# A two-block transformer layer on one core: another order of work at four norms, and the second attention's last product in three fp32r products

## The chip, the cores and the metric

The kernel runs on one core of one Trainium2 chip, as one launch. The metric is the device time of that launch in microseconds (us); the median of three runs of the kernel before is 2761.93 us (2761.17 to 2762.11). Everything is computed on 256 tokens with a model width of 2048.

## The reference, cut to what matters

Two blocks follow each other. Each mixes tokens, adds a normed result to the residual x, and runs a gated feed-forward (FFN). The norms and the second block's linear attention are what the change touches:

```
def rms_norm(x, g):                    # mean of squares over the 2048 features
    y = xf * lax.rsqrt(mean(xf * xf) + 1e-6);  return y * g
# first block
h = rms_norm(x, mix_pre_g); ... mixed = concat(o_da, o_hg) @ w_out
x = x + rms_norm(mixed, mix_post_g)
h = rms_norm(x, cross_pre_g); qx = h @ w_cq ...          # norm 1 (cq)
x = x + rms_norm(o @ w_co, cross_post_g)
h = rms_norm(x, ffn_pre_g); gate, up = h @ w_ffn_in      # norm 2 (Fg0)
x = x + rms_norm((silu(gate) * up) @ w_ffn_out, ffn_post_g)
# second block
h = rms_norm_2(x, norm_mix_pre); z = h @ w_in            # norm 3 (R0)
A = masked, decayed scores of q and k (gla);  o = A @ v  # the "second attention"
o = rms_norm_2(o, gla_norm) * silu(r); y_b = o @ w_branch_b
mixed = (gates0 * y_a + gates1 * y_b) @ w_out
x = x + rms_norm_2(mixed, norm_mix_post)
h = rms_norm_2(x, norm_ffn_pre); f = (silu(h @ wg) * (h @ wu)) @ w_ffn_down   # norm 4 (Hg0)
x = x + rms_norm_2(f, norm_ffn_post)
```

So four times a post norm is added to x and the new x is normed for the next projection: these four places are "the later norms" 1 to 4.

## The kernel before, in words

**The stream of weights.** All weights are cut into slots of 128 x 1024 numbers, in the order in which they are used. SyncE loads slot i into one of four RAW buffers; ScalarE copies it to RH as fp32r (the high part, `s_hi`); VectorE subtracts and writes the rest to RL (the low part, `s_lo_v`). For six slots (the second one, index 1, of cq, co0, co1, Fg0, R0 and Hg0) GpSimd makes the low part instead (`on_pool`). TensorE multiplies each slot in three fp32r products (low of tokens by high of weights, high by low, high by high): 12 matmuls of 512 columns for most slots. RH and RL have four buffers, so the high part of slot i can be made only when slot i-4 is multiplied. `upto(n)` on an engine means "do the slots up to n"; the engines run three slots ahead (LA).

**Order.** Each engine's instruction list is written out by hand in the functions `tensor`, `scalar`, `vector`, `gpsimd`; each engine works through its own list strictly in order and waits at semaphores. Work beside the stream is a "side task" with ticks in slots (`yield at`): `sides.behind(t)` emits all side work due up to tick t, after the engine's own work of that slot.

**A later norm n.** The last four slots of the projection before it (`tail_of`) are multiplied for token block b = 0 (tokens 0 to 127) and then for b = 1 (`by_token_halves`). When b = 0 is done, ScalarE squares its last quarter, VectorE makes the mean (`post_mean`), GpSimd the power -0.5, and VectorE adds four quarters of 512 features to x (`post_add`, `s_xv`). TensorE turns x over by transposes into eight steps (`half_turns`, steps 0 and 1 for b = 0, 2 and 3 for b = 1, both with features 0 to 1023; 4 to 7 with features 1024 to 2047 of both blocks). For each step ScalarE writes the high part of the turned x (`half_highs`, `s_nhi`) and VectorE the low part (`half_lows`, `s_nlo`). `by_token_head` multiplies the first four slots of the next projection, called f to f+3 below, in an order that follows these steps, and `rest_by_token` the slots f+4 to f+7, one after the other. On ScalarE, `row_task(n)` then squares x in four halves of 1024 (ticks f, f+1, f+2, f+2.5) for the norm's scale; by the lists, three of them stand ahead of the high part of slot f+6.

**The second attention's last product** (`gla_out_task`). Scores ATT2, AX2 and values V2 are plain fp32; eight outputs (4 heads, 2 token blocks) come from 12 fp32 matmuls of 512 columns, in two lumps in slots of R1. ScalarE and VectorE copy them out.

**Level tasks.** The causal decays of both attentions are made in levels L = 0, 1, 2, ... (`level_plan`): spans and factors on VectorE, exp on ScalarE, small products on TensorE (`e.mul`), a masked copy on VectorE (`e.take`).

Of the kernel before, what the change touches and what calls it, by code (L numbers as in the profile page):

```python
# [7 lines left out]
F32 = mybir.dt.float32  # L8
# [5 lines left out]
P = 128  # L14
D = 2048
T = 256
# [151 lines left out]
def build(nc, A, out, scratch):  # L168
    ctx = ExitStack()
    with ctx:  # L170
# [106 lines left out]
        on_pool = {i for n in ("cq", "co0", "co1", "Fg0", "R0", "Hg0") for i in groups[n][1:2]}  # L277
# [47 lines left out]
        s_sg = sem("branch_gate_ready")  # L325
        s_go, s_gov, s_goa = sem("gla_out_multiplied"), sem("gla_out_copied_by_vector"), sem("gla_out_copied_by_scalar")
# [33 lines left out]

        low_sum = {}
# [24 lines left out]
        NORM_BANKS = []  # L386
        for n, name in enumerate(NORMED):
            head = unit[name, 0]
            tail = unit[NORM_AFTER[n][-1], 0] if n else [6, 7]
            NORM_BANKS.append(head + [b for b in range(8) if b not in head + tail] + tail)  # L390
# [41 lines left out]
        GLA_END = last("V0")  # L432

# [9 lines left out]
        def level_plan(todo, at, period, fac, banks, base, squeeze):  # L443
# [3 lines left out]
            for L in todo:  # L447
# [9 lines left out]
                else:  # L457
                    e.mul, e.take = squeeze(at), squeeze(at + 2)
# [46 lines left out]
        V2 = U(0, 2).rearrange("p (b n) -> p b n", b=2)  # L505
# [59 lines left out]
        def tensor(g):  # L565
# [103 lines left out]
            def by_token_halves(name, H, L, n=None):  # L669
# [42 lines left out]
            def half_turns(n, s0, s1):  # L712


                for s in range(s0, s1):
# [6 lines left out]
                    for blk in range(cols.start // P, cols.stop // P):  # L722
                        g.wait_ge(s_xv, 8 * (n - 1) + 4 * blk + chunks[0] // 4 + 1)
# [5 lines left out]
            def by_token_head(name, H, L, n):  # L729
# [41 lines left out]
                rest_by_token(name, H, L, 8, lambda k: (s_nlo, 8 * n + k // 2 + 1))  # L771

            def rest_by_token(name, H, L, k, ready):
                banks = unit[name, 0]
                for i in groups[name][k // 2:]:
                    wait_low(i)
# [14 lines left out]

            def norm(n):
                banks = NORM_BANKS[n]

                def turn_over(i, blk):
                    if blk == 0:
                        for name in NORM_AFTER[n]:
                            if banks[i] in unit[name, 0]:
                                g.wait_ge(*free_of[name, 0][unit[name, 0].index(banks[i])])
                    g.wait_ge(s_xv, 8 * (n - 1) + 4 * blk + i // 2 + 1)  # L800
                    for c in range(2):
                        cc = 2 * i + c
                        t = turn(PS[:, banks[i], c * T + blk * P:c * T + blk * P + P], X[:, blk, cc * P:cc * P + P])
                    if blk:
                        t.then_inc(s_tr, 1)

                assert n not in HALVED
                for blk in range(2):
                    for i in range(8):
                        turn_over(i, blk)  # L810
# [224 lines left out]
            def gla_out_task():  # L1035
                at = lambda h, s: ATT2[:, (2 * h + s) * P:(2 * h + s) * P + P]
                yield GLA_OUT
                g.wait_ge(s_free_a, read_a["V3"])
                for j in range(2):
                    g.wait_ge(s_lv_v[j], gla_done[j][0])  # L1040
                for blk in range(2):
                    for h in range(4):
                        vs, o = slice(512 * h, 512 * h + 512), PS[:, 4 + h, :]
                        if blk == 0:
                            mm(o, at(h, 0), V2[:, 0, vs], True, True).then_inc(s_go, 1)
                        else:
                            if h % 2:
                                g.wait_ge(s_goa, h // 2 + 1)
                            else:
                                g.wait_ge(s_gov, h // 2 + 1)  # L1050
                            mm(o, at(h, 1), V2[:, 1, vs], True, False)
                            mm(o, AX2[:, h * P:h * P + P], V2[:, 0, vs], False, True).then_inc(s_go, 1)
                    yield GLA_OUT + 1
# [86 lines left out]
        def scalar(g):  # L1140
# [62 lines left out]
            def half_norm(n, half):  # L1203


                H, f = NORM_HOME[n][0], first(NORMED[n])
                upto(f + 1)
                if n == 2:
                    half(1, [2])
                g.wait_ge(s_slot, last(HOME_READ[n]) + 1)  # L1210
# [7 lines left out]
            def norm(n, H, next_slot):  # L1218
                gain = PRE_GAIN[n]
                g.wait_ge(s_slot, last(HOME_READ[n]) + 1)  # L1220
                for i in range(8):
                    if i == 2:
                        upto(next_slot + 1)
                    g.wait_ge(s_tr, 8 * (n - 1) + i + 1)
                    for c in range(2):
                        t = act(H[:, 2 * i + c, :], PS[:, NORM_BANKS[n][i], c * T:c * T + T], scale=gcol(gain, 2 * i + c))
                    t.then_inc(s_nhi, 1)
# [32 lines left out]
            def row_task(n):  # L1260
                at = first(NORMED[n]) + (0, 4)[n == 0]
                ss = stat(f"row_ssq{n}", 4).rearrange("p (b h) -> p b h", b=2)
                for q, (half, b) in enumerate(X_HALF):
# [5 lines left out]
                    else:  # L1269
                        g.wait_ge(s_xv, 8 * (n - 1) + 4 * b + 2 * half + 2)  # L1270
# [154 lines left out]

            def gla_out_task():
                ss = stat("gla_ssq", 8)
                for blk in range(2):
                    yield GLA_OUT + blk
                    for h in (1, 3):  # L1430
                        g.wait_ge(s_go, 4 * blk + h + 1)
                        act(O2[:, blk, h, :], PS[:, 4 + h, :]).then_inc(s_goa, 1)
# [24 lines left out]
            def mixed_task():  # L1457
                for j in range(4):
# [10 lines left out]
                          pool_task(), gla_out_task(), branch_gate_task(0), branch_gate_task(1), mixed_task(), row_task(4), hidden_task(0), hidden_task(1))  # L1469
# [156 lines left out]
            for j in range(4):  # L1626

                def second_values(banks):
                    for x in range(2):
                        g.wait_ge(s_lv_v[x], gla_done[x][0])  # L1630
# [1014 lines left out]
```

## Time and profile before

| | |
|---|---|
| median of 3 runs | 2761.93 us |
| the profiled execution | 2762.22 us |
| its span | 2760.4 us |
| TensorE matmul busy | 2739.2 us, 99% |
| VectorE busy | 1813.2 us, 66% |
| ScalarE busy | 1338.3 us, 48% |
| GpSimd busy | 76.0 us, 3% |
| granted TensorE clock, mean | 0.998 of 2.4 GHz |

The span is what lies between the first and the last instruction of the execution; the execution's own time is 1.8 us longer. TensorE is the engine to look at: the other engines matter only where TensorE waits for them. A timeline row gives start, length, instruction and count, and in square brackets the idle time of the engine ahead of it with what ended it.

### The profile page before, as it was taken

How to read it: one execution, taken by the hardware profiler on the slowest of the kernel's cores; microseconds unless marked ns; L12 is line 12 of the kernel's file. 1: busy time of each engine (PE TensorE's matmuls, PEld its weight loads, DVE VectorE, ACT ScalarE, POOL GpSimd, SP SyncE). 2: the span in 40 equal slices, each digit the busy share in tenths (PEclk: the TensorE clock that was granted, in tenths of full speed). 3: DMA queues.
4: the chain of work that ended last, by engine and by line, in shares of the span. 5: the costliest groups of instructions: out<-in, count | busy, mean ns of one | idle time of the engine just before them, and what ended most of it. 6: DMA issues, size and time to landing. Idle time of an engine off the chain costs nothing.

```text
span 2760.4 us, 35257 instructions
## 1 busy us (share of the span) xinstructions
PE 2739.2 (99%) x14278; PEld 2272.6 (82%) x14278; DVE 1813.2 (66%) x2294; ACT 1338.3 (48%) x1604; POOL 76.0 (3%) x61
## 2 busy tenths in 40 slices
PE   9999999999999999999999999999999999999998
PEld 7888887888888888887888887888888888888887
DVE  6778865575556655766679754868667546656575
ACT  5666544664444434445545545544454444443443
POOL 0000000110000000000002000000010000000000
PEclk9999999999999999999999999999999999999999
DMA  8555455556655665554655555565655555565655
GB/s 324 195 165 175 155 186 181 174 186 203 193 190 190 199 195 192 194 188 161 223 177 179 182 190 195 189 212 182 206 192 189 198 193 194 186 202 189 197 190 160
DMA packets 145540, 529.21 MB, mean 192 GB/s; under 512 B 16305, under 2 KB 16737, under 8 KB 144737
## 3 DMA queue, kind: packets, MB, share of 16 engines
q1 hardware_dynamic: 142528, 514.71, 57.0%
q0 software_dynamic: 2560, 12.07, 1.2%
q8 instruction: 113, 1.85, 0.3%
q14 instruction: 51, 0.41, 0.0%
q10 hardware_dynamic: 288, 0.16, 0.0%
HBM read 524.78 MB, written 2.11 MB: 191 GB/s over the span
## 4 chain that ended last, share of the span: by engine, by line
PE 95%; DVE 2%; ACT 2%; issue 1%; DMA 0%; POOL 0%; DVEq 0%; SPq 0%; POOLq 0%; ACTq 0%
PE PS L568 95%; PE PS L571 1%; ACT RH L1145 1%; DVE RL L1652 1%; ACT A_HL L1145 1%; DVE AR L1652 0%; ACT SP L1145 0%; DVE AR L2136 0%; DMA RAW<-in_stream 0%; DVE X L1658 0%; DVE A_HL L1658 0%; ACT B_HL L1145 0%; DVE AR L1891 0%; POOL ST L2406 0%; DVE AR L1655 0%
## 5 line engine op out<-in xcount | busy, mean ns | idle before, releaser
L1652 DVE TENSOR_TENSOR RL<-RAW,RH 128x1024 fp32r<-128x1024 f32 x954 | 1159.3, 1225 | 837.3 <-ACT RH L1145 835.2
L1145 ACT ACTIVATE RH<-RAW 128x1024 fp32r<-128x1024 f32 (+1 forms) x962 | 1013.9, 1057 | 1129.5 <-PE PS L568 1101.6
L568 PE MATMUL PS<-RH,A_HL 128*128 128x512 f32 x4096 | 1271.9, 391 | 4.3 <-ACT A_HL L1145 1.4
L568 PEld LDWEIGHTS PS<-RH,A_HL 128*128 128x128 f32 x4096 | 768.5, 188 | 168.4 <-issue 6.5
L568 PE MATMUL PS<-RH,B_HL 128*128 128x512 f32 x2624 | 810.6, 390 | 0.4 <-DVE RL L1652 0.3
L568 PE MATMUL PS<-RL,A_HL 128*128 128x512 f32 x2048 | 793.4, 390 | 0.0
L568 PEld LDWEIGHTS PS<-RH,B_HL 128*128 128x128 f32 x2624 | 492.5, 188 | 103.9 <-DVE RL L1652 1.3
L568 PE MATMUL PS<-RL,B_HL 128*128 128x512 f32 x1312 | 509.0, 389 | 0.0
L568 PEld LDWEIGHTS PS<-RL,A_HL 128*128 128x128 f32 x2048 | 384.9, 188 | 78.8 <-issue 0.5
L568 PEld LDWEIGHTS PS<-RL,B_HL 128*128 128x128 f32 x1312 | 246.2, 188 | 50.6
L568 PE MATMUL PS<-A_HL,RH 128*128 128x512 f32 (+1 forms) x912 | 221.5, 394 | 2.0 <-DVE A_HL L1658 2.0
L568 PEld LDWEIGHTS PS<-A_HL,RH 128*128 128x128 f32 (+1 forms) x912 | 165.6, 189 | 36.0 <-issue 3.2
L2112 DVE STREAM_TRANSPOSE AR<-AR 32x256 f32<-32x256 f32 x352 | 153.3, 436 | 4.9
L568 PEld LDWEIGHTS PS<-A_HL,RL 128*128 128x128 f32 (+1 forms) x912 | 118.0, 192 | 6.4 <-DVE RL L1652 0.8
L568 PE MATMUL PS<-A_HL,RL 128*128 128x256 f32 (+1 forms) x912 | 122.7, 287 | 0.0
L1652 DVE TENSOR_TENSOR AR<-PS,AR 128x512 f32<-128x512 f32 (+2 forms) x106 | 77.2, 740 | 44.2 <-ACT AR L1145 26.3
L1652 DVE TENSOR_TENSOR AR<-AR 128x512 f32<-128x512 f32 (+3 forms) x145 | 100.9, 733 | 0.4
L2406 POOL TENSOR_TENSOR ST<-ST,NEG 128x1 f32<-128x1 f32 (+2 forms) x21 | 26.1, 1241 | 2020.9 <-DVE ST L1658 1725.7
L1145 ACT ACTIVATE AR<-PS,ST 128x512 f32<-128x512 f32 (+1 forms) x82 | 50.6, 666 | 57.9 <-PE PS L568 55.9
L1145 ACT ACTIVATE AR<-AR 128x1024 f32<-128x1024 f32 (+2 forms) x64 | 65.0, 1029 | 13.4 <-DVE AR L1652 9.0
L1145 ACT ACTIVATE AR<-PS 128x512 f32<-128x512 f32 (+2 forms) x48 | 31.6, 665 | 73.3 <-PE PS L568 69.2
L568 PEld LDWEIGHTS PS<-AR 128*32 128x32 f32 (+5 forms) x1938 | 48.7, 119 | 14.6 <-issue 10.5
(117 smaller groups left out, 832.5 us busy)
## 6 DMA issues: line engine op xcount, KB each, us to landing
RAW<-in_stream SPq DMA_DIRECT2D x959, 512.0 KB, 4.2
X<-in_x SPq DMA_DIRECT2D x4, 512.0 KB, 7.0
AR<-in_mem SPq DMA_DIRECT2D x4, 512.0 KB, 6.8
AR<-in_mem_turned SPq DMA_DIRECT2D x4, 512.0 KB, 5.1
AR<-in_b_branch_gates POOLq DMA_DIRECT2D x4, 512.0 KB, 6.3
AR<-in_b_branch_gates POOLq DMA_DIRECT2D x2, 1024.0 KB, 8.6
out_x<-X SPq DMA_DIRECT2D x8, 256.0 KB, 2.7
AR<-in_x_turned SPq DMA_DIRECT2D x3, 512.0 KB, 8.3
```

The source lines that it names most:

```text
L568: return g.matmul(o, l, r, start=start, stop=stop, skip_group_check=True)
L571: return g.transpose(o, i, ident)
L1145: return g.activation(o, i, f, bias=bias, scale=scale, accum_out=accum)
L1652: return g.tensor_tensor(o, a, b, f)
L2112: t = g.transpose(dst[32 * fq:32 * fq + 32, :, :, tq, :], src[32 * tq:32 * tq + 32, :, :, fq, :])
L2406: return g.tensor_tensor(o, i, NEG[:, 0:k], ALU.pow)
```

## The change

- **Norms, TensorE.** The transposes of steps 4 to 7 no longer stand together in the head: steps 4 and 5 come late in the head, steps 6 and 7 between slots f+4 and f+5. The order of the head's products changes; at norm 3 steps 0 and 1 come one slot later.
- **Norms, ScalarE.** The first high parts no longer wait for the end of wo3 (norm 1) but for its head. The square of the last quarter of b = 1 comes between the high parts of slots f+2 and f+3 (norm 3: behind both). The high parts of steps 4 to 7 were one run behind slot f+5; now step 4 stands behind slot f+4, steps 5 to 7 behind slot f+5.
- **Norms, VectorE.** The additions to x are cut into first two quarters, third and last, with weights' low parts between; at norm 3 quarters of both blocks alternate.
- **GpSimd** makes low parts in co0 and co1 only; the four others go to VectorE.
- **Second attention.** Scores and values are split into high and low (in B_HL), and each fp32 matmul becomes three fp32r matmuls: 36 in all, head by head, in slots of V1, V2, V3 and R1.
- **Level L = 0**: `e.mul` one tick later, `e.take` half a tick later.
- **mixed_task**: the last two groups of VectorE's 32 x 32 transposes at ticks 2 and 3 instead of 1.5 and 2.

```diff
-        on_pool = {i for n in ("cq", "co0", "co1", "Fg0", "R0", "Hg0") for i in groups[n][1:2]}
+        on_pool = {i for n in ("co0", "co1") for i in groups[n][1:2]}
...
+        def quarter_added(n, b, c):
+            order = [(k, q) for k in range(2) for q in range(4)]
+            if n == 3:
+                order = [(0, 0), (0, 1), (1, 0), (1, 1), (0, 2), (1, 2), (0, 3), (1, 3)]
+            return 8 * (n - 1) + order.index((b, c)) + 1
...
-        HOME_READ = [None, "wo3", "cq", "Fu10", "yb3"]
+        HOME_READ = [None, head_of("wo3")[-1], last("cq"), last("Fu10"), last("yb3")]
...
-                    e.mul, e.take = squeeze(at), squeeze(at + 2)
+                    e.mul, e.take = squeeze(at + 1), squeeze(at + 2.5)
...                                          # tensor, by_token_halves and by_token_head
-                        if n in HALVED and b and i == tail_of(name)[2]:
+                        if n in HALVED and b and i == tail_of(name)[2 + (n == 3)]:
                             half_turns(n, 0, 2)
...
                 highs(0, range(4))
-                low_tokens(0, range(4))
-                half_turns(n, 2, 3)
-                low_weights(0, range(2))
+                low_tokens(0, range(2))
+                if n != 3:
+                    half_turns(n, 2, 3)
+                low_tokens(0, range(2, 4))
+                low_weights(0, range(1))
+                if n == 3:
+                    half_turns(n, 2, 3)
                 half_turns(n, 3, 4)
+                low_weights(0, range(1, 2))
+                highs(1, range(4))
+                low_tokens(1, range(4))
+                low_weights(1, range(2))
                 low_weights(0, range(2, 4))
-                for ms in (range(2), range(2, 4)):
-                    if ms[0]:
-                        half_turns(n, 4, 8)
-                    highs(1, ms)
-                    low_tokens(1, ms)
-                    low_weights(1, ms)
+                half_turns(n, 4, 6)
+                low_weights(1, range(2, 4))
...                                          # rest_by_token
                 for i in groups[name][k // 2:]:
+                    if k == 10:
+                        half_turns(n, 6, 8)
                     wait_low(i)
...                                          # scalar, half_norm
                 half_highs(n, H, 0, 2)
+                upto(f + 2)
+                if n == 3:
+                    upto(f + 3)
+                half(1, [3])
                 upto(f + 3)
-                half(1, [3])
                 half_highs(n, H, 2, 4)
+                upto(f + 4)
+                half_highs(n, H, 4, 5)
                 upto(f + 5)
-                half_highs(n, H, 4, 8)
+                half_highs(n, H, 5, 8)
...                                          # vector, half_norm (after)
+                for step in ("early", "sum", "mean", "first_quarters"):
+                    half(0, step)
+                upto(f)
+                if n != 3:
+                    half(0, "last_gain")
+                    half(0, "third_quarter")
+                    half(0, "last_quarter")
+                    half(1, "early")
+                half_lows(n, 0, 1)
                 half(1, "sum")
+                half_lows(n, 1, 2)
+                if n == 3:
+                    half(0, "last_gain")
                 half(1, "mean")
                 half(1, "first_quarters")
+                upto(f + 2)
+                half_lows(n, 2, 4)
                 upto(f + 3)
+                if n == 3:
+                    half(0, "third_quarter")
+                half(1, "third_quarter")
                 upto(f + 4)
+                half_lows(n, 4, 5)
+                half(1, "last_gain")
+                if n == 3:
+                    half(0, "last_quarter")
+                half(1, "last_quarter")
+                half_lows(n, 5, 6)
+                upto(f + 5)
+                half_lows(n, 6, 8)
...                                          # tensor, gla_out_task (after)
+                def product(o, c, h, vb, start, stop):
+                    high, low, cs = V2H[h % 2][:, vb, :], V2L[h % 2][:, vb, :], slice(c * P, c * P + P)
+                    mm(o, ATT_L[:, cs], high, start, False)
+                    mm(o, ATT_H[:, cs], low, False, False)
+                    return mm(o, ATT_H[:, cs], high, False, stop)
+                for h in range(4):
+                    yield GLA_HEAD[h]          # last(f"V{h}") + 2.5
+                    g.wait_ge(s_v2l, h + 1)
+                    g.wait_ge(s_atl, 2)
+                    product(PS[:, b, :], 2 * h, h, 0, True, True).then_inc(s_go, 1)
+                    product(PS[:, b + 1, :], 2 * h + 1, h, 1, True, False)
+                    product(PS[:, b + 1, :], 8 + h, h, 0, False, True).then_inc(s_go, 1)
...                                          # vector, mixed_task
-                        yield last(f"yb{j}") + (0.5, 1, 1.5, 2)[fq]
+                        yield last(f"yb{j}") + (0.5, 1, 2, 3)[fq]
```

## Rows read from the trace of the kernel before

**Rows 1.** The page: busy time of each engine, and the chain that ended last.
```profile
PE 2739.2 (99%) x14278; PEld 2272.6 (82%) x14278; DVE 1813.2 (66%) x2294; ACT 1338.3 (48%) x1604; POOL 76.0 (3%) x61
PE 95%; DVE 2%; ACT 2%; issue 1%; DMA 0%; POOL 0%; DVEq 0%; SPq 0%; POOLq 0%; ACTq 0%
```
**Rows 2.** Busy time in stretches: engines' busy us (count), clock, DMA share, GB/s.
```profile
600.00:800.00 200.00, 200.00 (x884) 165.69 (x884) 116.81 (x131) 88.30 (x87) 0.00 (x0) 1.00 0.60 193
```
**Rows 3.** Timeline of TensorE at norm 4.
```profile
2039.51 1.91 PE L571 MATMUL PS<-EYE,X 128*128 128x128 f32 x16
2041.18 2.07 PE L568 MATMUL PS<-RH,B_HL 128*128 128x512 f32 x8
...
2049.90 0.50 PE L568 MATMUL PS<-RH,B_HL 128*128 128x512 f32 x1 [0.30 <-DVE RL L1652]
```
**Rows 4.** Timeline of ScalarE at norm 4.
```profile
2041.23 3.01 ACT L1145 ACTIVATE B_HL<-PS,GC 128x256 fp32r<-128x256 f32 x8
2044.08 1.11 ACT L1145 ACTIVATE SP<-X 128x1024 f32<-128x1024 f32 x1
...
2047.54 1.04 ACT L1145 ACTIVATE RH<-RAW 128x1024 fp32r<-128x1024 f32 x1
```
**Rows 5.** Timeline of VectorE at norm 4.
```profile
2048.62 1.23 DVE L1652 TENSOR_TENSOR RL<-RAW,RH 128x1024 fp32r<-128x1024 f32 x1 [2.18 <-ACT RH L1145]
```
**Rows 6.** Norm 1, timeline of TensorE.
```profile
476.69 1.17 PE L568 MATMUL PS<-RH,A_HL 128*128 128x512 f32 x4 [1.43 <-ACT A_HL L1145]
478.56 0.71 PE L568 MATMUL PS<-RH,A_HL 128*128 128x512 f32 x2 [0.70 <-ACT RH L1145]
497.75 0.50 PE L568 MATMUL PS<-RH,A_HL 128*128 128x512 f32 x1 [0.28 <-DVE RL L1652]
```
**Rows 7.** Norm 2, timeline of TensorE.
```profile
578.35 0.50 PE L568 MATMUL PS<-RH,A_HL 128*128 128x512 f32 x1 [0.28 <-DVE RL L1652]
```
**Rows 8.** Norm 3, timeline of TensorE.
```profile
1288.94 0.63 PE L571 MATMUL PS<-EYE,X 128*128 128x128 f32 x4 [2.17 <-DVE X L1658]
1306.44 0.50 PE L568 MATMUL PS<-RH,A_HL 128*128 128x512 f32 x1 [0.27 <-DVE RL L1652]
```
**Rows 9.** Busy time in the stretch behind that wait.
```profile
1290.00:1293.30 3.30, 3.30 (x12) 2.62 (x11) 3.08 (x8) 1.88 (x7) 0.00 (x0) 0.50 0.47 158
```
**Rows 10.** A low part on GpSimd, and one on VectorE that runs beside it.
```profile
472.70 3.79 POOL L2382 TENSOR_TENSOR RL<-RAW,RH 128x1024 fp32r<-128x1024 f32 x1 [2.42 <-ACT RH L1145]
473.05 1.22 DVE L1652 TENSOR_TENSOR RL<-RAW,RH 128x1024 fp32r<-128x1024 f32 x1
```
**Rows 11.** Second attention: fp32 products by form, first lump's timeline, the last score copy.
```profile
L568 PE MATMUL PS<-AR,SP 128*128 128x512 f32 x16 | 7.7, 592 | 0.0
L568 PE MATMUL PS<-AR,SM 128*128 128x512 f32 x8 | 4.1, 592 | 0.0
1693.74 3.59 PE L568 MATMUL PS<-AR,SP 128*128 128x512 f32 x8
1697.40 0.40 PE L568 MATMUL PS<-RL,A_HL 128*128 128x512 f32 x1
L1925 DVE COPY SM<-PS x1: 420/420/420, 1613.7 to 1613.7; 128x256 f32<-128x256 f32 x1
```
**Rows 12.** First attention, level 0: TensorE's wait, and what VectorE made.
```profile
256.03 0.75 PE L568 MATMUL PS<-AR 128*32 128x32 f32 x64 [1.25 <-DVE AR L1652]
255.20 0.69 DVE L1652 TENSOR_TENSOR AR<-AR,RR 128x512 f32<-128x512 f32 x1
```
**Rows 13.** From yb3 to W0: VectorE, ScalarE, TensorE.
```profile
1949.52 3.60 DVE L2136 STREAM_TRANSPOSE AR<-AR 32x256 f32<-32x256 f32 x8
1953.15 1.06 ACT L1145 ACTIVATE A_HL<-AR 128x1024 fp32r<-128x1024 f32 x1 [2.76 <-DVE AR L2136]
1956.56 1.22 DVE L1652 TENSOR_TENSOR A_HL<-AR,A_HL 128x1024 fp32r<-128x1024 f32 x1
1957.92 0.47 PE L568 MATMUL PS<-RH,A_HL 128*128 128x512 f32 x1 [0.50 <-DVE A_HL L1652]
```

More of the change, by code:

```diff
@@ L359, in build @@
             free_of[n, 0] = [(s_free_a, i + 1)] * 2
+        for j in range(4):
+            free_of[f"V{j}", 0] = free_of[f"V{j}", 0] + [(s_v2l, j + 1)]
         low_sum = {}
@@ L432, in build @@
         GLA_END = last("V0")
+        SCORES = GLA_END - 1
+        GLA_HEAD = [last(f"V{h}") + 2.5 for h in range(4)]
         def hg_at(t):
@@ L790, in rest_by_token @@
                     sides.behind(i)
[L792 to L810, printed above, removed]
             def normed(n):
@@ L1209, in half_norm @@
                     half(1, [2])
-                g.wait_ge(s_slot, last(HOME_READ[n]) + 1)
+                g.wait_ge(s_slot, HOME_READ[n] + 1)
                 half_highs(n, H, 0, 2)
+                upto(f + 2)
+                if n == 3:
+                    upto(f + 3)
+                half(1, [3])
                 upto(f + 3)
-                half(1, [3])
                 half_highs(n, H, 2, 4)
+                upto(f + 4)
+                half_highs(n, H, 4, 5)
                 upto(f + 5)
-                half_highs(n, H, 4, 8)
[L1218 to L1227, printed above, removed]
+                half_highs(n, H, 5, 8)
             def first_norm():
@@ L1628, in second_values @@
                 def second_values(banks):
-                    for x in range(2):
-                        g.wait_ge(s_lv_v[x], gla_done[x][0])
-                    coled(V2[:, :, 512 * j:512 * j + 512], 3)(banks)
+                    if j > 1:
+                        g.wait_ge(s_go, 2 * j - 2)
+                    coled(V2H[j % 2], 3)(banks)
                 through(f"V{j}", second_values)
@@ L1704, in through_halves @@
                 upto(tail_of(name)[-1])
-                half(0)
-                upto(tail_of(name)[-1] + 1)
                 if n in HALVED:
                     half_norm(n, half)
-                else:
-                    half(1)
+                    return
+                half(0, "all")
+                upto(tail_of(name)[-1] + 1)
+                half(1, "all")
             def half_lows(n, s0, s1):
@@ L2193, in tokens, with half @@
                     through(f"{name}{c}", evict)
-                def half(b, step="all"):
+                def half(b, step):
                     done = 8 * i + (4 + 2 * b if name == "co" else 5 + b)
-                    if step in ("all", "early"):
+                    if step == "early":
                         if name == "co":
@@ L2205, in half @@
                             post_part(n, 1, ssq)
-                    if step in ("all", "mean"):
+                    if step == "mean":
                         g.wait_ge(s_tsq, done + 2)
@@ L2250, in add_each, with half @@
                             gain(j - 1)
-                    def half(k, step="all"):
+                    def half(k, step):
                         if step in ("all", "sum"):
@@ L2261, in half @@
                             add(k, unit[f"{tag}o2_3", 0])
-                        if step in ("all", "last_quarters"):
+                        if step in ("all", "last_gain"):
                             g.wait_ge(s_gb, (48, 80)[f])
@@ L2353, in vector, with low_values @@
                 through(f"ya{j}", gated)
-            for n in ("V0", "V1", "V2", "V3", "R1", "R2", "R3"):
+            for j in range(4):
+                def low_values(banks, p, low):
+                    g.wait_ge(s_free_a, read_a[f"V{j}"])
+                    for b in range(2):
+                        t = stt(V2L[j % 2][:, b, :], PS[:, banks[b], :], row_col[3][:, b:b + 1], V2H[j % 2][:, b, :].bitcast(F32),
+                                ALU.mult, ALU.subtract)
+                    t.then_inc(s_v2l, 1)
+                through(f"V{j}", low_values)
+            for n in ("R1", "R2", "R3"):
                 through(n)
```

106 lines of the change are left out of this document (44 added, 62 removed).

## The prediction, made before the changed kernel ran

> **What bounds the kernel.** I read the page first: TensorE is busy 99% of the span, and the chain that ended last lies 95% on it [rows 1]. So the time is TensorE's work plus the places where it waits, and I looked up each wait of TensorE and then, for each, the list of the engine that it waits for. In a stretch without waits 884 matmuls of 512 columns take 200 us [rows 2]: 0.226 us each, 2.72 us for a slot of 12. The reader is to see in the norm rows that waits are small (0.3 to 2.2 us) and that all four norms have one in common: just ahead of slot f+6 TensorE waits for RL, 0.3 us of idle time [rows 3] (with the restart 0.45 us over the normal step: at norm 4 the last matmul before it starts at 2049.21 by the timeline, the next at 2049.90, against 0.226). The change has to be judged by what it does to these waits.
>
> **The wait at slot f+6, all four norms.** Before, ScalarE writes the high parts of steps 4 to 7 in one run of 3.01 us, then squares x (three of them from 2044.08 until RH starts at 2047.54: 3.46 us, 1.15 each), then makes RH of f+6 (1.04 us), and VectorE makes RL from it (2048.62 + 1.23 = 2049.85); TensorE goes on at 2049.90 [rows 3, 4, 5]. That whole chain starts from the transposes at 2039.51, a full head half ahead of slot f+4.
>
> After, the transposes of steps 6 and 7 stand between slots f+4 and f+5. ScalarE's list is in order, so the squares, and RH of f+6 behind them, cannot start before the high parts of 6 and 7. From the end of the transposes: 0.55 us until the high part of step 6 is done, 0.75 for that of step 7 (3.01 us / 4 [rows 4]), 3.46 for three squares, 1.05 for RH, 0.05, 1.2 for RL: 7.05 us. TensorE has only slot f+5, 2.72 us, to do in that time. It waits 4.3 us where it waited 0.45. This sum doesn't depend on what came ahead of it: the chain starts from TensorE's own transposes. What covered RH of f+6 was the distance from transposes to f+6 (10.4 us at norm 4), and that cover is now 2.7 us. Behind RH of f+6 stand the fourth square and RH of f+7: 2.2 us and 1.2 for RL against slot f+6's 2.72, ready just in time after the wait. SyncE's load of slot f+10 waits for RL of f+6; TensorE needs it four slots (10.9 us) later, so that stays hidden.
>
> **The rest of each norm, followed on all lists.** I carried the three lists on with durations of before: RH 1.0, RL 1.15 start to start, four high parts of 128 columns 1.05 and four low parts 1.05, an addition to x 0.68, TensorE to ScalarE 0.2, and 1.66 us for 16 transposes (2039.51 to the next product at 2041.18 [rows 3]).
>
> Norm 4, end of W3 at 2029.86: the square of b = 1 now stands ahead of RH of f+3, which is done at 2032.1 instead of 2031.3. TensorE's fourth pair of high products waits 1.0 us (0.2 before). The low parts, quarters of x and RL of f+1 (done 2035.1, on VectorE now) come in time for the new order. Slot f counts as multiplied at 2040.6; RH of f+4 41.65, RL 42.95; steps 4 and 5 are turned at 42.6, high part 43.15, low part 44.0: slot f+4 starts at 44.1 (TensorE was ready at 43.55), ends 46.85, transposes to 47.7, slot f+5 to 50.45, wait to 54.8. Before: 2049.90 with the same work done. So **+5.0 us**.
>
> Norm 1: the wait of 1.43 us for the high parts goes [rows 6], since they no longer wait for the end of wo3. What is late next is RH of f+3, done 477.5 instead of 479.4 (the high parts start at 472.6): one wait of 1.15 us in place of 1.43, 0.70 and 0.24. Then 0.5 at slot f+4 and the 4.3: slot f+6 at 500.15 against 497.75, **+2.4**. Norm 2 has no such gain to take: RH of f+3 moves from 559.7 to 560.5, slot f+4 starts at 572.85, f+6 at 583.5 against 578.35 [rows 7], **+5.1**. Norm 3 had a wait of 2.17 us for x, for whose b = 1 the mean stood behind other work on VectorE, and 3.4 us at half clock behind it [rows 8, 9]. With the transposes later and x in another order I find waits of 0.5, 0.5 and 0.4 us, slot f+4 at 1296.15, 0.35 us at f+5 for RL, 3.9 us at f+6: 1306.85 against 1306.44, **+0.4**. Sum of norms **+12.9 us**.
>
> Bounds: if an error of 1 us sits in the head of each norm, the sum is 9 to 17. The removal of GpSimd's four low parts is in these numbers (1.15 us of VectorE each). The page "GPSIMD Engine Reference" of the Trainium skill, in its comparison and limits, says that GpSimd shares its SBUF interfaces with VectorE and contends with VectorE instructions that have two SBUF inputs; by that, VectorE would gain here. The trace gives VectorE 1.22 us beside a running GpSimd instruction, the same as alone, and 3.79 to GpSimd [rows 10]: only GpSimd pays, and the sum gets nothing from it.
>
> **The clock.** At norm 3 the idle 2.17 us were followed by 3.4 us at a granted 0.50, 1.2 GHz, where 12 matmuls took 3.30 us [rows 8, 9]. Norm 1's 1.43 + 0.70 + 0.24 us had no such fall. A wait of 4.3 us in one piece is well above both, so I take one fall behind each of the four. One costs half of 3.4 us: 1.7, four **+6.8 us** (between 0 and 13, two stretches each). The fall that norm 3 had is already in its +0.4. The Trainium skill, page "TensorE: Matmul & The Clock Gate", in its table of terms, prices throttled time by one minus the clock ratio: half of it here, as the row gives.
>
> **Second attention.** Removed: 12 fp32 matmuls, 24 records [rows 11]. The first lump holds TensorE from 1693.74 to 1697.40 with one normal matmul in it: 3.43 us for 8 records; 16 more are 6.86: 10.3 us. Added: 36 fp32r matmuls x 0.226 = 8.15. **-2.1 us** (between -2.6 and +1, if loading the new weights hid less well). Added on ScalarE: two copies, 1.7 us, once; on VectorE 1.9 us once and four times 1.4 us for the values' low parts. Both have 1.5 us or more of idle time per slot there, and a head's low part is ready some 3 us after its slot ends, 6.8 us ahead of its product. If that cover were gone it would be 1 to 2 us a head. What is queued behind ScalarE's wait for the levels is RH of the next slots; the levels' last score copy is at 1613.7 [rows 11], in V0's fourth slot, ahead of the tick of the copies two slots on.
>
> **Level 0.** TensorE waited 1.25 us for VectorE's product [rows 12], ready 255.9. One tick (one slot, 2.7 us) later there is nothing to wait for: **-1.3** (0 to -1.4).
>
> **From yb3 to W0.** VectorE works without a break up to A_HL's last low part, 1956.56, and TensorE waits 0.50 us for it [rows 13]. Two ticks' shift puts one weight low part (1.15 us) ahead of the last four transposes. ScalarE's A_HL, RH behind it, RL from that and the low part all start that much later: **+1.1** (0 to +1.3). For the three earlier columns nobody waits.
>
> **Sum.** 12.9 + 6.8 - 2.1 - 1.3 + 1.1 = +17.4. On the profiled execution's 2762.2 (span 2760.4 and 1.8 around it) 2779.6; this execution lies 0.3 above the median of the runs, so 2779.3, **2779 us**.
>
> **Rivals.**
> A. The waits come, but the clock stays up: 2779.3 - 6.8 = 2772.5. For it: norm 1's broken gaps left the clock at full. Against: one gap of 2.17 us did not.
> B. Each wait costs two slow stretches, or 4 us waits delay the next loads too: up to +6.8, 2786.
> C. Not slower. The waits ahead of f+6 stay at 0.45 us, since the squares turn out not to stand between TensorE's late transposes and RH of f+6. Then four times 3.8 us (3.5 at norm 3) and the clock's 6.8 go: 2779.3 - 14.9 - 6.8 = 2757.6, 0.16% faster, within what is told from no change, carried by norm 3, second attention and level 0. It decides from the point where ScalarE finishes the squares within 2.7 us of the transposes. For it: only that the lists are read by me; before, the rows show exactly the order highs, square, square, square, RH [rows 4], and nothing in the diff moves `row_task`.
> D. The change doesn't do what it says at the heads: RH of f+3 behind the square costs more than found (1 us a norm): that is inside the forecast's own range.
> The Trainium skill's same page on the clock says that the default state is the throttled one and that activity releases it; by that A is the less likely, and its chance is small beside the forecast's.
>
> **Chances.** Forecast 0.58, A 0.20, B 0.08, C 0.14. A measurement of this kernel tells 0.2% (5.5 us) from no change. Slower by more than that: 0.86; within 0.10; faster 0.04, the last two out of C (and a part for each out of its bounds). The range that holds 8 in 10 takes in A and B, and leaves C out: 2768 to 2787.
>
> **What would show it.** Right: at each of the four norms one TensorE wait of about 4 us for DVE RL just ahead of slot f+6 (near 498, 585, 1315 and 2064 in the new time), with ACT's three SP<-X rows behind the highs of steps 6 and 7, and a granted 0.5 behind it; 36 rows of 0.226 us in V1 to R1; no wait at 256; a wait of 1.6 us ahead of W0's chunk 12. Wrong: slot f+6 starting within 0.5 us of the end of f+5, or the norms' waits elsewhere.

## The result, and the profile after

The changed kernel took 2780.03 us (median of 4 runs, 2778.85 to 2780.95) against 2761.84 us for the kernel before on the same chip (2761.17 to 2762.11): ratio 1.0066, 95% interval 1.0054 to 1.0078. It is slower, by 18.2 us; the forecast was 2779.

The page of the kernel after, busy time and chain, which answers to [rows 1]. TensorE is busy 4 us longer in a span that is 18.7 us longer (2779.1 against 2760.4), so most of the loss is idle time. (Busy time is a net figure: products at half clock add to it, and the second attention's products take less.)
```profile
PE 2743.3 (99%) x14290; PEld 2279.0 (82%) x14290; DVE 1822.7 (66%) x2308; ACT 1340.3 (48%) x1606; POOL 60.7 (2%) x57
PE 97%; ACT 1%; issue 1%; DVE 1%; DMA 0%; DVEq 0%; POOL 0%; SPq 0%; POOLq 0%; ACTq 0%
```
What TensorE waited for in the kernel after: total us, times, longest. In the kernel before, the line for RL had 1.1 us in four waits, none over 0.3 [rows 3, 6, 7, 8].
```profile
PE PS L577 <- DVE RL L1648: 16.1, 4, 4.1
PE PS L577 <- DVE A_HL L1654: 3.9, 5, 1.6
PE PS L577 <- ACT RH L1140: 3.4, 6, 0.8
PE PS L577 <- DVE A_HL L1648: 1.6, 1, 1.6
```
The four waits for RL are the first products of slot f+6 at norms 1 to 4. Timeline of TensorE, after; they answer to the last rows of [rows 6, 7, 8, 3]:
```profile
498.97 0.79 PE L577 MATMUL PS<-RH,A_HL 128*128 128x512 f32 x1 [4.07 <-DVE RL L1648]
...
587.02 0.80 PE L577 MATMUL PS<-RH,A_HL 128*128 128x512 f32 x1 [4.06 <-DVE RL L1648]
...
1318.80 0.50 PE L577 MATMUL PS<-RH,A_HL 128*128 128x512 f32 x1 [3.89 <-DVE RL L1648]
...
2059.27 1.04 PE L580 MATMUL PS<-EYE,X 128*128 128x128 f32 x8
2060.06 0.47 PE L577 MATMUL PS<-RH,B_HL 128*128 128x512 f32 x1
...
2067.14 0.57 PE L577 MATMUL PS<-RH,B_HL 128*128 128x512 f32 x1 [4.07 <-DVE RL L1648]
```
What stands in those 7.08 us (2060.06 to 2067.14) on ScalarE, after, norm 4 [rows 4]: four high parts, three squares, and only then RH of f+6.
```profile
2059.91 1.57 ACT L1140 ACTIVATE B_HL<-PS,GC 128x256 fp32r<-128x256 f32 x4 [2.83 <-PE PS L580]
2061.35 1.08 ACT L1140 ACTIVATE SP<-X 128x1024 f32<-128x1024 f32 x1
...
2064.79 1.04 ACT L1140 ACTIVATE RH<-RAW 128x1024 fp32r<-128x1024 f32 x1
```
And VectorE, after, norm 4 [rows 5]:
```profile
2065.86 1.22 DVE L1648 TENSOR_TENSOR RL<-RAW,RH 128x1024 fp32r<-128x1024 f32 x1 [3.42 <-ACT RH L1140]
```
Busy time in the stretches behind the four waits, after (PE, PEld, DVE, ACT, POOL, clock, DMA share, GB/s). The granted clock is 0.50 in all four, over about 6.8 us at norms 1 and 2 and 3.4 us at norms 3 and 4. At its norms the kernel before had one such stretch of 3.4 us, at norm 3 [rows 9].
```profile
497.40:504.10 6.70, 5.13 (x12) 4.07 (x13) 4.95 (x6) 4.13 (x6) 1.62 (x1) 0.50 0.54 167
586.10:592.80 6.70, 5.78 (x14) 4.52 (x15) 4.59 (x6) 3.68 (x6) 1.62 (x1) 0.50 0.60 185
1320.00:1323.30 3.30, 3.30 (x10) 2.56 (x9) 2.09 (x4) 1.00 (x3) 2.13 (x2) 0.50 0.81 264
2067.50:2070.80 3.30, 3.30 (x9) 2.65 (x8) 2.92 (x5) 2.21 (x3) 1.38 (x1) 0.50 0.69 180
```
TensorE's other wait that grew stands ahead of W0's last slot [rows 13]:
```profile
1969.96 0.47 PE L577 MATMUL PS<-RH,A_HL 128*128 128x512 f32 x1 [1.57 <-DVE A_HL L1648]
```
To find where the time went, the same matmul (by its number in TensorE's list) is compared in both profiled executions; "by place" below is the step of that difference across a stretch. At a norm it is taken from ahead of the norm to behind the half clock that follows it.

| place | predicted, with the clock | measured |
|---|---|---|
| level 0 | -1.3 | -1.3 |
| norm 1 | +2.4 + 1.7 | +5.0 |
| norm 2 | +5.1 + 1.7 | +7.8 |
| norm 3 | +0.4 + 1.7 | +2.3 |
| second attention | -2.1 | -2.2 |
| yb3 to W0 | +1.1 | +1.0 |
| norm 4 | +5.0 + 1.7 | +6.8 |
| rest | 0 | -0.6 |
| sum | +17.4 | +18.8 |

### The profile page after: what moved, and what is told of

Its sections match the earlier page's. It is cut to its first block, busy times and chain, and to the rows that moved or that the text cites. A ratio compares the mean times of both kernels' runs of the same rounds, so it can differ in the third digit from the quotient of the medians.

```text
span 2779.1 us, 35306 instructions
## 1 busy us (share of the span) xinstructions
PE 2743.3 (99%) x14290; PEld 2279.0 (82%) x14290; DVE 1822.7 (66%) x2308; ACT 1340.3 (48%) x1606; POOL 60.7 (2%) x57
## 4 chain that ended last, share of the span: by engine, by line
PE 97%; ACT 1%; issue 1%; DVE 1%; DMA 0%; DVEq 0%; POOL 0%; SPq 0%; POOLq 0%; ACTq 0%
PE PS L577 96%; PE PS L580 1%; ACT A_HL L1140 0%; ACT RH L1140 0%; ACT SP L1140 0%; DVE RL L1648 0%; DMA RAW<-in_stream 0%; ACT B_HL L1140 0%; DVE X L1654 0%; DVE A_HL L1654 0%; DVEq L170 0%; DVE A_HL L1648 0%; POOL ST L2429 0%; DVE AR L1648 0%; POOLq L170 0%
## 5 line engine op out<-in xcount | busy, mean ns | idle before, releaser
L577 PEld LDWEIGHTS PS<-AR 128*32 128x32 f32 (+5 forms) x1938 | 48.6, 119 | 12.9 <-issue 8.8
```

The costliest lines, as they stand in the source:

```text
L577: return g.matmul(o, l, r, start=start, stop=stop, skip_group_check=True)
```

## The experiments

All are built on the kernel after unless they say otherwise. "Before" is the kernel before, timed in turn with them on the same chip: 2761.61 us for the first four, 2761.54 for the next four, 2761.73 for the last two. The kernel after was not timed again with them, and its own four runs spread over 2.1 us; so a difference to it of 1 or 2 us is read by place, from the profiled executions.

**1. square_per_slot: what fills ScalarE's list ahead of f+6.**
```diff
-                    yield at + ((0, 1, 2, 2.5)[q] if n else q + q // 2)
+                    yield at + ((2.5, 3.5, 4.5, 5.5)[q] if n else q + q // 2)
...   # the tasks that use the squares' sum come 1.5 to 2.5 slots later
```


> The changed kernel with one thing more: at the four later norms ScalarE's squares of x stand one per slot behind the high parts of f+6 to f+9 (ticks f+2.5, 3.5, 4.5, 5.5 instead of f, f+1, f+2, f+2.5), and what uses the norm's scale comes 1.5 to 2.5 ticks later. Theory (the squares between the late transposes and RH of f+6 make the four waits of 4.07, 4.06, 3.89 and 4.07 us, and the waits make the clock fall): from the end of the transposes 1.25 us of high parts, 1.05 RH, 1.25 RL is 3.6 us against slot f+5's 2.7, so each wait falls to 0.9 us; none is followed by a granted 0.5; 2780.0 - 12.8 - 8.9 for the clock = 2758, about 0.15% under the kernel before. Rival 1 (the wait is RAW's load or VectorE's list, not the squares): waits of 4 us stay, 2780. Rival 2 (the wait only moves to f+7 or f+8, since ScalarE's work behind the late transposes is the same): four waits of 3 us in all at f+6 to f+9, 2770 or more.

Measured 2758.79 us (11 runs, 2758.66 to 2759.36), ratio to before 0.999 (0.9981 to 0.9999): 21.2 us less than after. At f+6 the waits are 0.67, 0.67, 0.55 and 0.67 us; here at norm 4, and none of the four is followed by the half clock.
```profile
2046.57 0.50 PE L577 MATMUL PS<-RH,B_HL 128*128 128x512 f32 x1 [0.67 <-DVE RL L1648]
```
So the squares between the late high parts and RH of f+6 are the loss. The time also says what the new order of the norms is worth without them: by place -0.8, +1.7, -2.3 and +1.7 us at norms 1 to 4, together +0.3. Of the 2.8 us by which this kernel is under before, 2.5 are level 0 and second attention less W0 (-1.3 - 2.2 + 1.0).

**2. busy_wait: how much of it is the clock.** 18 products of 512 columns into a free bank, one row of 0.226 us each, fill TensorE's wait ahead of f+6.
```diff
+                    if k == 12:
+                        for _ in range(18):
+                            mm(PS[:, HALF_BANKS[n][1][0], :], H[:, 0, 0:P], both, True, True)
```


> The changed kernel with 18 matmuls of 512 columns into a free bank ahead of slot f+6 at the four norms, whose results nobody reads: 4.07 us of work in the place of the wait. Theory (the waits themselves cost 16 us, and the half clock behind them 2.6, 2.9, 1.7 and 1.7 us = 8.9): TensorE has no idle stretch there, the clock stays at 1.00 behind all four, slot f+6 starts within 0.3 us of where it did, 2771. Rival (the falls come from the heads with their transposes and small waits, not from the 4 us of idle): the granted 0.5 stays, 2780 or, as the extra matmuls delay nothing, the same time.

Measured 2772.29 us (5 runs, 2772.19 to 2772.55), ratio 1.0039 (1.0026 to 1.0052), with no half-clock stretch between start and end. Slot f+6 starts where it did, within 0.1 us by place, and the kernel is 7.7 us faster than after: that is the clock's share. By place the four stretches give 2.4, 2.7, 1.3 and 1.6 us, 8.0 together; another 0.7 us of this one execution lies in its first 20 us, where the edit does nothing. Of the 21.2 us of experiment 1, the other 13.5 are the waits themselves.

**3. turns_together: the transposes' place.** Steps 4 to 7 together in the head, none between f+4 and f+5.
```diff
-                half_turns(n, 4, 6)
+                half_turns(n, 4, 8)
...
-                    if k == 10:
-                        half_turns(n, 6, 8)
```


> The changed kernel with the transposes of steps 6 and 7 put back beside steps 4 and 5 (late in the head); ScalarE's and VectorE's lists stay. Theory (the distance from the transposes to slot f+6 is the cover of the squares): ScalarE still makes high 4, RH f+5, high 5 to 7, three squares, RH f+6 behind the transposes, 8.6 us and RL 1.25; TensorE has 0.9 + 2.7 + 2.7 us of work and 0.5 us of wait at f+4: a wait of 2.5 to 3 us ahead of f+6, 1.2 to 2.6 us less in each norm; the clock falls behind some of them or none: 2761 to 2772. Rival (the place of the transposes does not matter, the new order of the head does): 2780 with waits of 4 us.

Measured 2768.52 us (10 runs, 2767.76 to 2769.55), ratio 1.0024 (1.0015 to 1.0033). The time lies in the expected range, the place does not: there is no wait at f+6 at all. TensorE now waits for the last quarter of x, which VectorE adds only behind slot f+4's low part. The row of norm 4 (the others had 2.57, 2.57 and 2.75 us), and the wait table:
```profile
2048.00 0.88 PE L580 MATMUL PS<-EYE,X 128*128 128x128 f32 x6 [2.57 <-DVE X L1652]
```
```profile
PE PS L580 <- DVE X L1652: 10.5, 4, 2.8
```
Each of the four was followed by 3.4 us at half clock. So putting the transposes back is worth 11.5 us and not all of the loss: the change put x's last quarters late, and TensorE, turning earlier, now waits 2.6 us for x where it waited 4.1 us for RL. The squares are what can give way without a price (experiment 1).

**4. old_mixed: the ticks of the 32 x 32 transposes.**
```diff
-                        yield last(f"yb{j}") + (0.5, 1, 2, 3)[fq]
+                        yield last(f"yb{j}") + (0.5, 1, 1.5, 2)[fq]
```


> The changed kernel with the transposes of the mixed branches at ticks 0.5, 1, 1.5, 2 as before. Theory (one low part of weights ahead of the last four transposes delays ScalarE's high part, RH, RL and the low part of A_HL by 1.1 us): the wait of TensorE in W0 goes from 1.57 to 0.50 us, 1.0 us less in all, 2779.0; rival (the longer wait comes from the shorter second attention or anything else upstream): 1.57 us stay.

Measured 2779.01 us (2 runs), ratio 1.0062 (1.0044 to 1.008): 1.0 us under after, and the wait ahead of W0's last slot is near the 0.50 us of [rows 13] again. By place W0 gives 0.65 us back, since TensorE's products just ahead of that wait start 0.45 us later than in after; in experiment 5, which has the same edit, W0 gives 1.1.
```profile
1967.97 0.47 PE L577 MATMUL PS<-RH,A_HL 128*128 128x512 f32 x1 [0.46 <-DVE A_HL L1648]
```

**5. rh_first: a version that beats both.** Experiments 1 and 4, and RH and RL of f+6 ahead of the high and low parts of steps 6 and 7; steps 4 and 5 turned one run of products earlier.
```diff
                 upto(f + 5)
-                half_highs(n, H, 5, 8)
+                half_highs(n, H, 5, 6)
+                upto(f + 6)
+                half_highs(n, H, 6, 8)
...
-                low_weights(0, range(2, 4))
                 half_turns(n, 4, 6)
+                low_weights(0, range(2, 4))
```


> One square per slot, and three things more: ScalarE makes RH of f+6 (and VectorE its low part) ahead of the high parts of steps 6 and 7, TensorE turns steps 4 and 5 over ahead of the low weights of f+2 and f+3, and the mixed branches' ticks are those of before. Theory: what is left of the wait ahead of f+6 (0.67, 0.67, 0.55, 0.67 us) goes, since RH of f+6 no longer waits for the late transposes at all; the wait of 0.57 us at f+4 shrinks to 0.2; W0's wait goes from 1.56 to 0.5: 2758.8 - 2.6 - 1.5 - 1.0 = 2753.7, 8 us under the kernel before. Rival (the low parts of steps 6 and 7, now behind a weight's low part on VectorE, are late for f+6 and f+7): waits move there, 2757 or more.

Measured 2752.86 us (6 runs, 2752.24 to 2753.35), ratio to before 0.9969 (0.9957 to 0.9981): 8.7 us under before and 27 under after. No wait at f+6. In this kernel's ScalarE at norm 4, RH slots stand between the squares, so none is more than one square late:
```profile
2038.09 1.57 ACT L1140 ACTIVATE B_HL<-PS,GC 128x256 fp32r<-128x256 f32 x4 [2.29 <-PE PS L580]
2039.54 1.08 ACT L1140 ACTIVATE SP<-X 128x1024 f32<-128x1024 f32 x1
...
2040.58 1.07 ACT L1140 ACTIVATE RH<-RAW 128x1024 fp32r<-128x1024 f32 x1
2041.52 1.07 ACT L1140 ACTIVATE SP<-X 128x1024 f32<-128x1024 f32 x1
```

**6. fp32_product: the second attention as before.** The whole of that edit undone (`gla_out_task`, the scores' and values' halves), the rest of the change kept.
```diff
-                    mm(o, ATT_L[:, cs], high, start, False)
-                    mm(o, ATT_H[:, cs], low, False, False)
-                    return mm(o, ATT_H[:, cs], high, False, stop)
+                            mm(o, at(h, 1), V2[:, 1, vs], True, False)
+                            mm(o, AX2[:, h * P:h * P + P], V2[:, 0, vs], False, True).then_inc(s_go, 1)
```


> The changed kernel with the second attention's last product as before (12 fp32 matmuls in two lumps, V2 by one copy). Theory: the step is worth what TensorE's time of the products differs by, 10.3 - 8.15 us: 2780.0 + 2.1 = 2782.1, and between ya3 and G10 the trace shows 2.1 us more than the changed kernel. Rival (splitting scores and values costs ScalarE or VectorE what TensorE gains, or frees banks later): within 1 us of the changed kernel.

Measured 2781.31 us (2 runs), ratio 1.0073 (1.0054 to 1.0091). By place the stretch costs 2.17 us more than in after. The whole time shows less, +1.3 us over after's median, and +0.3 in the profiled executions: this one lost 0.7 us less in its first 20 us and had half the slow stretch at norm 1. The rows of the kernel after are nine fp32r products for each head, four times:
```profile
1669.71 2.20 PE L577 MATMUL PS<-B_HL 128*128 128x512 f32 x9
```

**7. square_late: the square of block b = 1 behind RH of f+3.**
```diff
-                upto(f + 2)
-                if n == 3:
-                    upto(f + 3)
+                upto(f + 3)
                 half(1, [3])
-                upto(f + 3)
```


> The changed kernel with ScalarE's square of the last quarter of b = 1 behind RH of f+3 at all four norms (as before, and as norm 3 still has it). Theory: the wait ahead of f+3's high product (0.73, 0.82 and 0.71 us at norms 1, 2 and 4) goes, and comes back ahead of step 2's transposes, since x of b = 1 is 0.5 to 1 us later: slot f+4 starts within 0.5 us of where it did, 2780 less 0 to 1.5. Rival (the square's place costs the full 0.7 us three times, as I put into my sum at 1.0 us a norm): 2777.9 or less.

Measured 2781.42 us (2 runs), ratio 1.0073 (1.0055 to 1.0092): 1.4 us over after's median, where up to 1.5 less was expected. The profiled executions differ by 0.4; by place f+4 starts 0.02 to 0.15 us later than in after, so nothing is won. The wait for RH of f+3 went and came back a few products later, for x: 0.49, 0.56 and 0.56 us at norms 1, 2 and 4 (norm 3 has the edit already). At norm 4 the kernel after had 0.71 for RH there; the row of this kernel:
```profile
2045.92 0.63 PE L580 MATMUL PS<-EYE,X 128*128 128x128 f32 x4 [0.56 <-DVE X L1652]
```

**8. pool_back: GpSimd's four low parts again.**
```diff
-        on_pool = {i for n in ("co0", "co1") for i in groups[n][1:2]}
+        on_pool = {i for n in ("cq", "co0", "co1", "Fg0", "R0", "Hg0") for i in groups[n][1:2]}
```


> The changed kernel with the second slot of cq, Fg0, R0 and Hg0 on GpSimd again (3.8 us there, 1.2 on VectorE). Theory: VectorE's low part of f+1 has room in the new order, slot f+4 waits for RH of f+4 and a high part, not for VectorE's length, so nothing moves: 2780.0 within 0.5, less 1 us at norm 3 at most, whose TensorE may wait for RL of f+1. Rival (VectorE is what sets the heads): up to 1.15 us per norm faster, 2775.4; second rival (GpSimd's 3.8 us are late for the product of f+1 or slow VectorE): slower by 1 to 4 us.

Measured 2785.14 us (2 runs), ratio 1.0087 (1.0068 to 1.0105): 5.1 us over after. My theory missed by that much. By place, up to slot f+6: +1.2 at norm 1, +1.5 at norm 2, 0 at norm 3, +1.3 at norm 4, 4.1 together. The half clock adds nothing to that: it is 3.4 us where after had 6.8 at norm 2, and 6.8 where after had 3.4 at norm 4. The two profiled executions differ by 3.8 us; what the medians add to it is not accounted for. At norm 4 GpSimd runs as VectorE's second pair of additions begins. GpSimd and VectorE of this kernel:
```profile
2040.99 2.47 POOL L2405 TENSOR_TENSOR RL<-RAW,RH 128x1024 fp32r<-128x1024 f32 x1 [2.38 <-ACT RH L1140]
```
```profile
2038.65 1.41 DVE L1654 SCALAR_TENSOR_TENSOR X<-AR,ST,X 128x512 f32<-128x512 f32 x2 [0.70 <-POOL ST L2429]
...
2041.72 2.96 DVE L1654 SCALAR_TENSOR_TENSOR X<-AR,ST,X 128x512 f32<-128x512 f32 x2
```
Two additions take 1.41 us alone and 2.96 here. Listed one by one, it is only the first of the two that is slow. It takes 2.30 us and ends at 2044.02, 0.56 us after GpSimd's instruction; the second takes 0.74 as ever:
```profile
2041.72 2.30 DVE L1654 SCALAR_TENSOR_TENSOR X<-AR,ST,X 128x512 f32<-128x512 f32 x1
2043.94 0.74 DVE L1654 SCALAR_TENSOR_TENSOR X<-AR,ST,X 128x512 f32<-128x512 f32 x1
```
It is the same at norms 1 and 2 (2.30 and 2.29 us, then 0.74). At norm 3 no addition comes beside GpSimd, and the step is 0. x is 1.5 us late, and TensorE, 1.18 us at norm 4, waits for it:
```profile
2048.39 0.63 PE L580 MATMUL PS<-EYE,X 128*128 128x128 f32 x4 [1.18 <-DVE X L1654]
```

**9. before_nopool: the same edit alone, in the kernel before.**
```diff
-        on_pool = {i for n in ("cq", "co0", "co1", "Fg0", "R0", "Hg0") for i in groups[n][1:2]}
+        on_pool = {i for n in ("co0", "co1") for i in groups[n][1:2]}
```


> The kernel before, with the weights' low parts of slots cq 1, Fg0 1, R0 1 and Hg0 1 made by VectorE instead of GpSimd; nothing else changed. Theory (GpSimd's pass over a weight slot slows the additions to x that VectorE does beside it): at norm 3 VectorE's four additions, which took 4.88 us with GpSimd running, take 2.7 to 2.9 us, so that x is ready some 2 us earlier less the 1.15 us of VectorE that the low part costs; TensorE's wait of 2.17 us for x goes to about 0.2 to 1, and the 3.4 us at half clock behind it go as well if the wait is short enough. At the other norms 0 to -0.5 us. Together 1.5 to 4 us faster: 2758 to 2760. First rival (my prediction: only GpSimd pays for the sharing, the time gets nothing from it): 2761.8, or with the extra 1.15 us of VectorE at places where it is late, up to 3 us slower. Second rival (GpSimd is slow but the additions were slow for another reason): additions at norm 3 still take 4 us or more.

Measured 2761.41 us (10 runs, 2760.93 to 2762.15), ratio 0.9999 (0.999 to 1.0008). The mechanism showed, the gain did not. At norm 3 of the kernel before, four additions took 4.88 us:
```profile
1277.43 4.88 DVE L1658 SCALAR_TENSOR_TENSOR X<-AR,ST,X 128x512 f32<-128x512 f32 x4 [0.75 <-POOL ST L2406]
```
Three of the four took 0.75 us; the last, behind the start of GpSimd's low part, took all of the excess and ended at 1282.31, 0.54 us after GpSimd (1278.96 + 2.81):
```profile
1279.42 2.89 DVE L1658 SCALAR_TENSOR_TENSOR X<-AR,ST,X 128x512 f32<-128x512 f32 x1
1278.96 2.81 POOL L2382 TENSOR_TENSOR RL<-RAW,RH 128x1024 fp32r<-128x1024 f32 x1 [1.66 <-ACT RH L1145]
```
Without GpSimd's low part they took 2.74, TensorE's wait for x fell from 2.17 [rows 8] to 1.74 us, and no half clock followed (by place -2.6):
```profile
1278.91 2.74 DVE L1658 SCALAR_TENSOR_TENSOR X<-AR,ST,X 128x512 f32<-128x512 f32 x4 [0.75 <-POOL ST L2406]
```
But at norms 1, 2 and 4 of the old order the 1.15 us more of VectorE came ahead of x, and TensorE waited for that: by place +0.6, +1.1 and +1.0. TensorE of the same kernel at norm 4, where the kernel before had no such row:
```profile
2033.84 0.63 PE L571 MATMUL PS<-EYE,X 128*128 128x128 f32 x4 [1.03 <-DVE X L1658]
```

**10. before_level: level 0's shift alone, in the kernel before.**
```diff
-                    e.mul, e.take = squeeze(at), squeeze(at + 2)
+                    e.mul, e.take = squeeze(at + 1), squeeze(at + 2.5)
```


> The kernel before, with the small products of level 0 one tick later and the masked copy half a tick later, as in the kernel after; nothing else changed. Theory: TensorE's wait of 1.25 us for VectorE near 255 goes, and every later product starts 1.3 us earlier: 2760.5, by place -1.3 from about 260 to the end. Rival: the later products delay the next level, and a wait of 0.5 to 1 us shows up behind it, so the time stays within 0.3 us of before.

Measured 2760.98 us (10 runs, 2759.12 to 2761.61), ratio 0.9998 (0.9988 to 1.0007), which alone would not tell it from no change. By place -1.32 at level 0, with no idle time ahead of the products, which answers to [rows 12]:
```profile
256.60 0.76 PE L568 MATMUL PS<-AR 128*32 128x32 f32 x64
```
In this execution 1.0 of it was given back at norm 1, by a half-clock stretch that the kernel before had not had there, about the same waits of 1.43 and 0.70 us [rows 6] (the stretch began at 475.97, behind the first and within the second); TensorE's timeline, and the clock of 476.1 to 479.3:
```profile
474.48 1.17 PE L568 MATMUL PS<-RH,A_HL 128*128 128x512 f32 x4 [1.43 <-ACT A_HL L1145]
476.34 4.46 PE L568 MATMUL PS<-RH,A_HL 128*128 128x512 f32 x12 [0.70 <-ACT RH L1145]
```
```profile
476.10:479.30 3.20, 2.96 (x7) 2.16 (x8) 2.33 (x6) 1.62 (x4) 0.55 (x1) 0.50 0.42 142
```

## Why the prediction was right, and where it was not

**The wait at f+6: right.** It is in the same place four times, 4.07, 4.06, 3.89 and 4.07 us of idle time (forecast 4.3, and 3.9 at norm 3); the chain from transposes to product took 7.08 us at norm 4 where the sum had 7.05. Experiment 1 took three squares out of that chain and with them the waits. What made this sum safe is that it starts at TensorE's own transposes, so no error made further up could enter it.

**The other norm terms: right.** With the clock's half taken out by the rows (next point), the four norms cost 21.9 - 8.9 = 13.0 us against 12.9. Norm 1 did trade 1.43 + 0.70 + 0.24 us for one wait of 0.73 (forecast 1.15), and TensorE waited 0.57 or 0.58 ahead of f+4 at all four norms. One price in it was no cost of its own: the square ahead of RH of f+3. Experiment 7 moved it away, and x was late next by nearly the same amount.

**The clock: right in kind, too small.** One stretch of 3.4 us behind each wait was forecast, a cost of 6.8 us together. At norms 1 and 2 the stretch was twice as long, what rival B had for all four. Half of TensorE's own time in them, 5.1, 5.9, 3.4 and 3.4 us, is 8.9 us; experiment 2 put it at 7.7 (8.0 by place) by a kernel that keeps TensorE at work there. "Half" itself is a little high: in the stretch at norm 3 a product of 512 columns starts every 0.43 us, against 0.226 at full clock, so 47% of the time is lost, which makes 8.4. That is the mis-sized term, by 0.9 to 2.1 us; the forecast was 1.0 us low, with 0.6 us of gains elsewhere ("rest") against it. Rival A (waits, but full clock, 2772.5) is what experiment 2 made by hand, 2772.29. It fell because the clock did fall; the step to it was priced right.

**Second attention, level 0, yb3 to W0: right.** Second attention -2.2 for -2.1; level 0 -1.3; W0 +1.0 for +1.1. The first two are shown alone, by place, by experiments 6 and 10. For W0 experiment 4 shows the longer wait gone (1.57 to 0.46 us), with 0.65 of it won by place.

**GpSimd: wrong.** "Only GpSimd pays, and the sum gets nothing from it" came from one pair in [rows 10]: there VectorE kept its 1.22 us and GpSimd took 3.79, against 2.40 in co0 and co1. Read one by one, the instructions of before and pool_back show what both sides pay: of two that meet, one goes first and the other ends a fixed time after it. Eight times VectorE had gone first, with a low part or an addition, and GpSimd's low part ended 2.22 to 2.28 us after VectorE's instruction, near the 2.40 it takes alone. Four times GpSimd went ahead of an addition to x, and the addition paid, ending 0.54 to 0.56 us after GpSimd's. The kind of instruction does not decide it alone: at norms 1, 2 and 4 of the kernel before the addition during which GpSimd's row starts kept its 0.75 us. What decides who goes first no experiment varied; the VectorE instructions that went first started ahead of GpSimd's row or at most 0.38 us behind it, and the held additions 0.46 us or more behind it. The row with the price was in the trace of before (4.88 us for four at norm 3) and I didn't look at it. The Trainium skill, page "GPSIMD Engine Reference", section "1. Specifications", names VectorE instructions with two SBUF inputs as those that contend; the trace agrees for the additions and for the weights' low parts, which both have two, and a TENSOR_TENSOR with one input in PSUM (AR<-PS,AR) kept its 0.68 us beside GpSimd at norm 4 of pool_back.

The total was right in spite of it by luck: I had carried every addition at its undisturbed 0.68 us, and those are the additions of a kernel without GpSimd's low parts. With GpSimd kept, the same hand-carried lists would have been about 4 us too low (experiment 8, by place). In the old order the same removal is worth nothing (experiment 9).

**Rival C** (2757.6, if the squares didn't stand there) is what experiment 1 made: 2758.8. So its price was right as well, and only the list decided between it and the forecast.

**Open.** Why some slow stretches are twice as long as others, behind waits that differ by 0.2 us at most. It is no property of norms 1 and 2: with the same waits of 3.9 to 4.1 us, the profiled executions of experiments 4 and 6 had 3.4 us at norm 1, and that of experiment 8 had 3.4 at norm 2 and 6.8 at norm 4. So part of the clock's cost differs from one execution to the next.

## What to carry to other kernels

When work of the engine that a bound engine waits for is in strict order, follow the list from the bound engine's own late output (here the last transposes) to the next thing it needs, and count everything in between, also what the edit doesn't touch: three unchanged squares were worth 21 us, with the clock, once the late high parts stood ahead of them. GpSimd taken off a job helps only the VectorE instructions that it held up, so look at the instructions beside it one by one: a mean over four (1.22 us) hid three of 0.75 and one of 2.89. Between late side work and an in-order supply, interleave one by one: one square per slot gave 21 us back, and the supply of f+6 ahead of the last side steps, with the earlier turns and the old transposes' ticks, another 6, which made a change 18 us slower into one 9 us faster.

## What the runs showed of the hardware

- When GpSimd's TENSOR_TENSOR of 128 x 1024 (2.40 us alone) meets a VectorE instruction with two operands in SBUF, one waits for the other. GpSimd's ended 2.22 to 2.28 us after VectorE's in eight cases of before and pool_back (then 2.42 to 3.87 us long); an addition to x (128 x 512, 0.75 us) ended 0.54 to 0.56 us after GpSimd's in four (then 2.29 to 2.89 us long).
- The half clock follows no fixed size of wait. Single waits of 1.03 to 1.57 us after the first 20 us left full clock. Waits of 1.43 and 0.70 us at norm 1 left full clock in two kernels' executions and saw 3.4 us at half clock in a third; 1.74 us at norm 3 left full clock, 2.17 half (before), four waits of 2.57 to 2.75 us half each time. Waits of 3.89 to 4.09 us saw half in all 20 cases of five kernels, 12 times for 3.4 us and 8 times for 6.8.
- In the first 15 us, where each execution waits 0.7 to 1.8 us near 9 us, 5 of 12 had such a stretch too, before and after among them.
- At half clock a product of 512 columns starts every 0.43 us, at full clock every 0.226.
- TensorE kept at work by products that nobody reads kept its full clock, worth 7.7 us over four waits.
